# Mixer projections as three fp32r products on split operands, their weights in pairs of ring slots

## The reference

```python
def hybrid_mixer(h, positions, layer, w_in, w_out, ...):
    (q1, q2, k1, k2, va, qb, kb, vb, ob, ib, fb, cq, ckv, kr) = jnp.split(h @ w_in, split_idx, axis=-1)
    out_a = diff_attention_group(q1, q2, k1, k2, va, ...)      # 4 heads, two softmaxes each
    out_b = mlstm_group(qb, kb, vb, ob, ib, fb, ...)           # conv, silu, gates, 6 heads
    out_c = mla_group(cq, ckv, kr, ...)                        # latents, rotary key, 6 heads
    return jnp.concatenate([out_a, out_b, out_c], axis=-1) @ w_out
# layer 0: dense SwiGLU (3584 wide); layer 1: top-2-of-8 expert SwiGLU
```

## Time and profile before

| | us |
|---|---|
| median of 3 runs | 1719.91 (1714.5 to 1721.17) |
| profiled execution | 1717.92 |
| its span in the trace | 1716.1 |
| PE busy | 1512.4 |
| DVE busy | 732.0 |
| ACT busy | 561.5 |
| PEld (weight loads into the array) | 1200.4 |
| POOL busy | 63.2 |

### The profile page before, as it was taken

The page is one execution under the profiler, slowest core; times in us unless marked ns, Lnnn a source line. Parts: engine busy times, 40 slices in busy tenths (PEclk is TensorE's granted clock), DMA queues, the critical chain, the costliest instruction groups (busy, mean ns, idle before and its releaser), DMA issues.

```text
span 1716.1 us, 29819 instructions
## 1 busy us (share of the span) xinstructions
PE 1512.4 (88%) x12054; PEld 1200.4 (70%) x12055; DVE 732.0 (43%) x1058; ACT 561.5 (33%) x777; POOL 63.2 (4%) x66
## 2 busy tenths in 40 slices
PE   5999999999999999856659999989997669999894
PEld 3868878999976776644447875489995458888552
DVE  2263265565534522300018871166772036666212
ACT  2134144444322321100016751056551035554101
POOL 0010000000010001000000000000000000000002
PEclk9999999999999999987879999989999779999997
DMA  9726467545352436699999999997577996555793
GB/s 357 273 95 239 191 245 276 201 176 203 138 192 74 173 147 274 273 424 423 425 425 426 400 378 403 425 369 286 236 279 313 424 424 260 221 221 221 311 426 149
DMA packets 74557, 488.85 MB, mean 285 GB/s; under 512 B 9792, under 2 KB 13920, under 8 KB 16544
## 3 DMA queue, kind: packets, MB, share of 16 engines
q1 hardware_dynamic: 72176, 479.94, 69.7%
q10 hardware_dynamic: 1648, 4.59, 0.8%
q0 software_dynamic: 576, 2.10, 0.4%
HBM read 482.66 MB, written 3.93 MB: 284 GB/s over the span
## 4 chain that ended last, share of the span: by engine, by line
PE 79%; DMA 10%; issue 5%; DVE 3%; ACT 2%; POOL 1%; SPq 1%; ACTq 0%; POOLq 0%; DVEq 0%
PE PG L1370 9%; PE PG L923 6%; PE Y L949 5%; PE PG L1414 5%; PE PG L1480 5%; PE TRB L1414 4%; DMA arena<-in_experts 4%; PE Y L1382 4%; PE Y L1442 4%; DMA ring<-in_experts 4%; PE Y L1211 3%; PE Y L957 3%; PE PG L925 3%; PE TRB L1420 3%; PE PG L1420 3%
## 5 line engine op out<-in xcount | busy, mean ns | idle before, releaser
L1370 PE MATMUL PG<-ring,mixT 128*32 128x128 f32 (+1 forms) x1920 | 116.3, 347 | 61.4 <-issue 56.9
L2381 DVE COPY arena<-TRB 128x64 f32<-128x64 f32 (+1 forms) x70 | 17.6, 251 | 340.3 <-PE TRB L1356 340.3
L1563 ACT ACTIVATE parts<-ring 128x2048 fp32r<-128x2048 f32 x84 | 157.2, 1901 | 4.8 <-PE PG L1480 4.8
L923 PE MATMUL PG<-h_parts,parts 128*128 128x512 f32 x432 | 152.8, 394 | 1.4 <-DVE arena L2260 1.4
L1370 PEld LDWEIGHTS PG<-ring,mixT 128*32 128x32 f32 (+1 forms) x1920 | 89.5, 136 | 91.7 <-issue 77.0
L1563 ACT ACTIVATE rope<-PG 64x128 f32<-64x128 f32 (+2 forms) x84 | 27.2, 324 | 376.5 <-PE PG L1370 352.6
L1370 PE MATMUL PG<-arena,mixT 128*32 128x128 f32 (+1 forms) x1664 | 103.6, 357 | 41.3 <-issue 41.3
L1370 PEld LDWEIGHTS PG<-arena,mixT 128*32 128x32 f32 (+1 forms) x1664 | 79.8, 141 | 69.1 <-issue 55.1
L925 PE MATMUL PG<-h_parts,parts 128*128 128x256 f32 x432 | 121.8, 282 | 0.0
L2245 DVE TENSOR_TENSOR parts<-ring,parts 128x2048 fp32r<-128x2048 f32 x42 | 95.1, 2289 | 32.7 <-ACT parts L1563 32.7
L2365 DVE TENSOR_TENSOR ring_parts<-ring,parts 128x2048 fp32r<-128x2048 f32 x42 | 95.0, 2286 | 22.4 <-PE Y L1433 19.4
(11 more groups left out here) (358 smaller groups left out, 2715.6 us busy)
## 6 DMA issues: line engine op xcount, KB each, us to landing
ring<-in_experts SPq DMA_DIRECT2D x168, 1024.0 KB, 12.2
arena<-in_experts SPq DMA_DIRECT2D x168, 1024.0 KB, 16.3
ring<-in_weights SPq DMA_DIRECT2D x116, 1024.0 KB, 6.3
ring<-in_weights SPq DMA_DIRECT2D x4, 512.0 KB, 4.2
ypairs<-hT ACTq DMA_DIRECT2D x3, 512.0 KB, 5.4
tok<-in_x SPq DMA_DIRECT2D x1, 1024.0 KB, 9.0
result<-scr SPq DMA_DIRECT2D x2, 512.0 KB, 2.6
ring<-in_weights SPq DMA_DIRECT2D x2, 432.0 KB, 6.5
```

Source lines behind the costliest of these rows:

```text
L923: mm(PG[:, m, :].rearrange("p (i t) -> p i t", i=2), w_hi[d % SPLITS][:, c], h_parts[:, :, k, :], start=(k == 0), stop=False, skip_group_c ...
L1370: last = mm(bank[i * n:(i + 1) * n, 0:width], xe[:, k, 0:n], w[k // 4][:, k % 4, i * width:(i + 1) * width], start=(k == 0), stop=(k == KD ...
L1563: return nc.scalar.activation(out_, in_, func, **kw)
```

## The change

h and the mixed rows are kept as hi and lo (h_parts; mix_hi and mix_lo use the same memory later), and the token rows tok become mtok, which uses hT's memory. ACT's shift now writes h_hi, and low_shifted on DVE writes h_lo. Each input and output weight takes two ring slots: SP loads it into the first, part on ACT copies it, rounded to fp32r, into the second ("hi"), and lower on DVE writes weight - hi over the loaded slot. SP skips the "hi" uses; part waits for the landing and for the last reader of the slot that it writes. The latent and the vb weights, which were cut by columns, are cut by rows, so that their products are 364 and 384 columns wide. PE does hi x hi and hi x lo, waits for the low weight, and does lo x hi. Row product D moves from behind the early output products to behind co. part and lower stand at fixed places in ACT's and DVE's programs.

```diff
-        uses.extend(("in", l, key) for key in W_IN_ORDER[a:b])
+        uses.extend((kind, l, key) for key in W_IN_ORDER[a:b] for kind in ("in", "hi"))
...
-        uses.extend(("out", l, c) for c in OUT_ORDER)
+        uses.extend((kind, l, c) for c in OUT_ORDER for kind in ("out", "hi"))
...
-W_IN_ORDER = [(COL_LAT, 256), (COL_LAT + 256, LATW - 256), (COL_Q, 256), (COL_Q + 256, 256), (COL_VA, 256),
+W_IN_ORDER = [(COL_LAT, LATW // 2), (COL_LAT + LATW // 2, LATW // 2), (COL_Q, 256), (COL_Q + 256, 256), (COL_VA, 256),
               (COL_QK, 256), (COL_QK + 256, 256), (COL_QK + 512, 256), (COL_OB, 256), (COL_OB + 256, 128),
-              (COL_VB, 256), (COL_VB + 256, 128)]
+              (COL_VB, BH * BD // 2), (COL_VB + BH * BD // 2, BH * BD // 2)]
+K_HALF = {W_IN_ORDER[0]: (COL_LAT, LATW, 0), W_IN_ORDER[1]: (COL_LAT, LATW, KD // 2),
+          W_IN_ORDER[10]: (COL_VB, BH * BD, 0), W_IN_ORDER[11]: (COL_VB, BH * BD, KD // 2)}
...
-            *[f"pt{u}" for u in range(6)], "rows2", "gt", "mt0", "cols2", "co0", "co1", "mt1", "mt2", "rows3",
+            *[f"pt{u}" for u in range(6)], "rows2", "gt", "mt0", "cols2", "co0", "co1", "rows3", "mt1", "mt2",
...
+        mix_hi, mix_lo = (h_parts[:, i, :, :] for i in range(2))
+        mtok = hT.rearrange("p k t -> p (k t)").rearrange("p (b d) -> p b d", b=TB)
...
-            eng.wait_ge(landed[slot_of[u]], 16 * (u // SLOTS + 1))
+            eng.wait_ge(landed[slot_of[u]], 16 * sum(x[0] != "hi" for x in uses[slot_of[u]:u + 1:SLOTS]))
+
+        def last_reader(kind, a, b):
+
+            if kind == "ada":
+                return tr_full, TR.full(("ada", a, b // 4))
+            if kind == "in" or kind == "hi" and b in IN_ITEM:
+                return pj_full, PJ.full((IN_ITEM[b], a))
+            if kind in ("out", "hi"):
+                return (y_full, 2 + a) if b == OUT_ORDER[-1] else (out_read, (D // SW - 1) * a + OUT_ORDER.index(b) + 1)
+            return split_lo, dense_use(kind, b) + 1
...
+                if kind == "hi":
+                    continue
                 if u >= SLOTS:
...
+                    hi, lo = proj_parts(l, key)
+                    hi_of(key)
                     for i in range(n):
-                        last = fm(bank[:, i * T:(i + 1) * T], s, i * P, P)
+                        for k in range(KD):
+                            for x in (h_hi, h_lo):
+                                mm(bank[:, i * T:(i + 1) * T], hi[:, k, i * P:(i + 1) * P], x[:, k, :],
+                                   start=(i == 0 and k == 0 and x is h_hi), stop=False, skip_group_check=True)
+                    lo_of(key)
+                    for i in range(n):
+                        for k in range(KD):
+                            last = mm(bank[:, i * T:(i + 1) * T], lo[:, k, i * P:(i + 1) * P], h_hi[:, k, :],
+                                      start=False, stop=(k == KD - 1), skip_group_check=True)
                     last.then_inc(pj_full, 1)
...
+                def latents():
+
+                    banks = [take_pj((f"lat{b}", l)) for b in range(TB)]
+                    halves = [proj_parts(l, key) for key in keys[0:2]]
+                    his, los = zip(*halves)
+                    h = KD // 2
+                    for b, bank in enumerate(banks):
+                        for k in range(KD):
+                            if b == 0:
+                                if k % h == 0:
+                                    hi_of(keys[k // h])
+                                pe.wait_ge(h_ready, KD * 2 * l + k + 1)
+                            mm(bank[:, 0:LATW], h_hi[:, k, b * P:(b + 1) * P], his[k // h][:, k % h, :],
+                               start=(k == 0), stop=False, skip_group_check=True)
...
+                    for b, bank in enumerate(banks):
+                        for k in range(KD):
+                            if b == 0:
+                                pe.wait_ge(h_lo_ready, KD * 2 * l + k + 1)
+                            last = mm(bank[:, 0:LATW], h_lo[:, k, b * P:(b + 1) * P], his[k // h][:, k % h, :],
+                                      start=False, stop=(k == KD - 1), skip_group_check=True)
+                        last.then_inc(pj_full, 1)
...
+                for key in keys[10:12]:
+                    hi_of(key)
+                    lo_of(key)
                 for b in range(TB):
                     bank = take_pj((f"vb{b}", l))
-                    tm(bank[:, 0:SW], s0, b, SW)
-                    tm(bank[:, SW:SW + P], s1, b, P).then_inc(pj_full, 1)
+                    tm(bank[:, 0:BH * BD], b, his, los).then_inc(pj_full, 1)
...
+                    hi, lo = proj_parts(l, c)
+                    late = tiles is MIX_LATE
+
+                    def product(w, x, k, j):
+                        return mm(Yk[:, 2 * c + j, :], w[:, k, j * P:(j + 1) * P], x[:, k, :],
+                                  start=(j == 0 and k == 0 and w is hi and x is mix_hi),
+                                  stop=(late and k == MIX_LATE[-1] and x is mix_lo), skip_group_check=True)
+
+                    hi_of(c)
                     for j in range(2):
                         for k in tiles:
-                            last = mm(Yk[:, 2 * c + j, :], ring[:, s, k, j * P:(j + 1) * P], mixT[:, k, :],
-                                      start=(j == 0 and k == 0), stop=(k == MIX_LATE[-1]), skip_group_check=True)
+                            product(hi, mix_hi, k, j)
+                    if not late:
+                        for j in range(2):
+                            for k in tiles:
+                                product(hi, mix_lo, k, j)
+                    lo_of(c)
+                    for j in range(2):
+                        for k in tiles:
+                            last = product(lo, mix_hi, k, j)
+                    if late:
+                        pe.wait_ge(mix_lo_ready, 2 * l + 2)
+                        for j in range(2):
+                            for k in tiles:
+                                last = product(hi, mix_lo, k, j)
                     return last
...
+            def part(l, key):
+                u, n = proj_use(l, key)
+                use_wait(ae, u)
+                if u + 1 >= SLOTS:
+                    ae.wait_ge(*last_reader(*uses[u + 1 - SLOTS]))
+                run(ring_parts[:, slot_of[u + 1], 0:n], ring[:, slot_of[u], :, :].rearrange("p k c -> p (k c)")[:, 0:n],
+                    ACT.Copy).then_inc(proj_hi, 1)
...
+                part(l, W_IN_ORDER[10])
                 at(2)
                 at(3)
+                part(l, W_IN_ORDER[11])
...
-                run(mixT[:, 0:2, :], bank.rearrange("p (a t) -> p a t", a=2), ACT.Copy, scale=gd[:, l:l + 1]).then_inc(free, 1)
+                run(mix_hi[:, 0:2, :], bank.rearrange("p (a t) -> p a t", a=2), ACT.Copy,
+                    scale=gd[:, l:l + 1]).then_inc(mix_hi_ready, 1)
+                part(l, OUT_ORDER[0])
                 ae.wait_ge(*tr_done("gt", l))
...
-            for third in ADA_START:
-                ada_rows(third)
+            ada_rows(ADA_START[0])
+            for key in W_IN_ORDER[0:2]:
+                part(0, key)
+            ada_rows(ADA_START[1])
             shift(0)
...
+            def lower(l, key):
+                u, n = proj_use(l, key)
+                ve.wait_ge(proj_hi, proj_index(l, key) + 1)
+                V.tensor_tensor(ring_parts[:, slot_of[u], 0:n], ring[:, slot_of[u], :, :].rearrange("p k c -> p (k c)")[:, 0:n],
+                                ring_parts[:, slot_of[u + 1], 0:n].bitcast(F32), ALU.subtract).then_inc(proj_lo, 1)
+
+            def low_shifted(n):
+                for k in range(KD):
+                    ve.wait_ge(h_ready, KD * n + k + 1)
+                    V.scalar_tensor_tensor(h_lo[:, k, :], hT[:, k, :], mod[:, n, k:k + 1], h_hi[:, k, :].bitcast(F32),
+                                           ALU.add, ALU.subtract).then_inc(h_lo_ready, 1)
...
+                lower(l, W_IN_ORDER[10])
                 negmaxes("c", 0, 1, 2, 3)
+                lower(l, W_IN_ORDER[11])
...
+                lower(l, OUT_ORDER[1])
+                for name, f, m in (("mt1", slice(5, 7), 2), ("mt2", slice(7, 8), 3)):
+                    bank, free = tr_item(name, l)
+                    n = f.stop - f.start
+                    ve.wait_ge(mix_hi_ready, 5 * l + m)
+                    V.tensor_tensor(mix_lo[:, f, :], bank[:, 0:n * T].rearrange("p (a t) -> p a t", a=n),
+                                    mix_hi[:, f, :].bitcast(F32), ALU.subtract).then_inc(free, 1)
...
+                late = [(name, j, f) for name, f0, n in (("mt3", 2, 2), ("mt4", 4, 1)) for j, f in enumerate(range(f0, f0 + n))]
+                turned = {name: tr_item(name, l)[0] for name in ("mt3", "mt4")}
+                for i, (name, j, f) in enumerate(late):
+                    last = V.scalar_tensor_tensor(mix_hi[:, f, :], turned[name][:, j * T:(j + 1) * T], gml[:, l, i:i + 1],
```

(37 more changed lines are left out.)

144 lines of the change are left out of this document (84 added, 60 removed).

## The result

| | before | after |
|---|---|---|
| median, us | 1719.65 (4 runs, 1714.5 to 1721.17) | 1738.62 (4 runs, 1735.97 to 1740.48) |
| profiled execution, us | 1717.92 | 1735.97 |
| its span | 1716.1 | 1734.2 |

The changed kernel is slower: ratio 1.0111, 95% interval 1.0094 to 1.0128, some 19 us where I had forecast 7 to 8. The time lies in my range, at its upper end.

What follows compares the result with a forecast made beforehand. PE was taken to bound the kernel, busy 88% of the span. Per mixer -16.7 + 4.0 + 2.1 + 8.6 + 2.4 = +0.4, with starts 3.4 and clock 3.6 in all +7.8: 1727 us, range 1706 to 1741.

Steps and rivals of the forecast that it cites:

- Products: PE in each mixer: three fp32r products at 0.119 us replace one fp32 product at 0.432 us, -16.7 us a mixer.
- Rival 4: Split products on PE take 0.144 us and not 0.119, so nothing is saved: 1760 us, chance 4%.
- Copies hidden: Input projections a0 to qk2: weight copies on ACT and subtractions on DVE cost nothing, with 1 to 4 us to spare.
- Rival 3: Copies taken as hidden come late on ACT, PE stops more often and the clock falls again: 1740 us, chance 22%.
- The starts: Mixer starts: latent weights' copy or subtractions delay the chain to hT, +1.4 us in mixer 0, +2.0 in mixer 1.
- Before vb: Ahead of vb products: aT late behind a vb copy, +1.65 us, then low vb weights late, +2.3; 4.0 a mixer.
- Loads behind vb1: Third row product's last weight gets its slot only when vb1 ends: +2.1 us; first output weight lands 16.8 us after vb1.
- ACT behind that load: ACT's copy of the first output weight holds up the gate exponentials: +8.6 us a mixer, the largest term, bounds 0 and 12.
- The end of the mixer: Early and late output products wait for low parts that DVE writes: +2.4 us a mixer.
- The loads for what follows: After the mixer: the dense stage's last ada weight lands at 4.3 us, asked at 4.8, and experts' loads are on time: nothing.
- The sum: Whole kernel: +0.8 us for two mixers, starts 3.4, clock 3.6, together +7.8; 1727 us from the median of 1719.91.
- The clock: One half-clock stretch of about 1.8 us per mixer, behind the 8.6 us stop: +3.6 us in all, bounds 0 and 9.

Runs made afterwards that it cites:

- Experiment 1: Changed kernel with ACT's copy of the first output weight behind the gate exponentials and its DVE subtraction behind the score products: 1717.03 us, ratio 1.0003.
- experiment 10: Changed kernel with seven edits of order, plus products of constants before the last start columns, both mixers' latents and the second pt: 1695.13 us, ratio 0.9864.
- experiment 2: Changed kernel with products of constants where PE waits before vb0, row product C, the third w and the dense stage's first row product: 1732.5 us, ratio 1.0088.
- experiment 6: Changed kernel with ACT's two aT evictions ahead of the first vb copy and low vb weights waited for only where used: 1736.0 us, ratio 1.0100.

## Why the prediction was right or wrong

**Products.** Right: -17.6 and -16.8 us of work for -16.7, at 0.121 us a product. Rival 4 is out.

**Copies hidden.** Right: from a0 to ob1 PE waits nowhere in either profile where it did not before. (Ahead of the prediction I gave the page's busy digits of ACT and DVE in the mixers as 0 to 3; they are 1 to 4 and 2 to 6. The windows of the earlier trace rows, on which the argument rests, are right.) Rival 3, which wanted late copies there, gave nearly the time that came (1740): its late copies did not come, its half clock behind more stops did. That the time lies in my range is luck in this sense: the range was held open by rival 3, not by the forecast's terms.

**The starts.** Mixer 0 +0.7 for +1.4, but +3.5 in the second profile, where the half clock ahead of it is 6.1 us and not 4.1. Mixer 1 +3.4 and, in the second profile, +1.7 for +2.0; 3.1 us of half clock lie in the first one's stretch.

**Before vb.** +1.65 and +2.3 forecast, the idle times are 1.34 and 1.69 us.

**Loads behind vb1.** C waits 5.1 us from vb1's end and not 4.3 (152.0 to 157.13; D's first weight is issued right behind it), +2.9 for +2.1. The output weight lands 18.5 us after vb1's end (170.5 - 152.0) for 16.8.

**ACT behind that load.** From C's end to co +9.4 and +9.3 us with the clock in it, for +8.6 and 1.8. ACT waits 6.12 and 6.56 us for the weight, where I wanted 7 to 9. Experiment 1 takes the stop away alone, and with it 18.6 of the 19 us.

**The end of the mixer.** The stops stand at 1.75 and 2.25 us, in both mixers; co to the end is 1.1 and 2.6 us shorter than before for -2.4.

**The loads for what follows.** Wrong in the first profile: "Nothing", since I took a lone load's 4.3 us. The last ada weight landed 7.6 us after its slot was free, with the transfers still busy (279 GB/s and more in each microsecond from 212 us on), and PE stood 2.81 us. In experiment 1 it came 5.1 us after, with a lull of 115 GB/s ahead of it. But in the second profile of the changed kernel the wait was 1.19 us and this stretch no longer than before, and in experiment 10 the weight came 7.9 us after, also with a lull of 115 GB/s ahead of it. What makes this load late stays open.

**The sum.** 1719.91 + 7.8 is 1727.7 and not 1727. Of the stretches at 528 and 706 us, which I priced at about 1.8, the windows give 1.7 and 1.3 us. Both are small beside the next.

**The clock: the step that failed.** "I count one per mixer, behind the 8.6 us stop: +3.6. Bounds 0 and, if the shorter stops do it too, 9." The first profile has eight stretches in the two mixers where before had one, 13.6 us more, and 4.8 between them; the second 18.8 more in the mixers. Both lie beyond my bound of 9. In the mixers alone the mis-sized term is 10.0 us short, of 10.3 between the forecast's +7.8 and the spans' +18.1; the other terms' errors (work -1.0, stops -2.8, the starts +0.7, the dense row product +2.5, the experts +0.9) nearly cancel, which is in part luck. In the second profile, whose span is 19.1 us above the one before, the term is 15.2 us short, and the others together were forecast 3.9 us too high.

I had looked at single stops and asked which is long enough. What the runs show is that stops of 1.3 to 3 us, each followed by dense work, also bring 0.50, at vb0, at C, at the latents, and not each time. The Trainium skill (TensorE: Matmul & The Clock Gate, "A second HAM failure mode: psum-queue depth-cycling") has a case where short idle times between groups of products, frequent enough, make the clock go down and up; the two traces agree with that rule rather than with the one I had taken, and it should have been the rival.

That the stop is the cause is shown for C and for the latents: there PE fell to 0.50 in all four cases of the changed kernel's two profiles, and stayed at 1.00 in both mixers where fillers stood in the stop (experiments 2 and 10). At vb0 it fell in three of four cases, and two with fillers are few to tell by.

The kernel before could have told me. I passed over a third stretch, in a row product at the start, behind a wait of 2.22 us. It costs 1.7 us and comes in both of its profiles:

```profile
32.17 5.35 PE L866 MATMUL TRB<-ring,ccol 128*32 128x256 f32 x64 [2.22 <-DMA ring<-in_weights]
...
33.00:36.00 3.00, 3.00 (x35) 1.91 (x28) 0.00 (x0) 0.00 (x0) 0.00 (x0) 0.50 1.09 343
```

And the stop before 17.28 us, which I took as a sign against, is there in all 13 profiles of these kernels at 2.75 or 2.76 us: in six of them PE falls to 0.50 within 2 us of it, in seven it does not.

How much of the time the half clock explains is less sure than its place in the account. Fillers took 11.3 us of it away and won 4 to 6 in the median (experiment 2), or 5.9 and won nothing (experiment 10). And experiment 1 brought the kernel back to the time of before with 20.6 us of it left.

What stays open: which of the short stops brings the half clock in a given execution. Two profiles of one program differ in it by up to 5.2 us within a mixer.

## What to carry to other kernels

Where an engine runs in order, a copy that waits for a load belongs behind everything that does not need it: one copy moved was worth 18.6 us, nearly the change's whole loss. Taking work off the engine that bounds gave it more stops here, and of the stops of 1.3 to 3 us many cost granted clock as well as idle time, so count every new stop of a microsecond or more at the clock it may leave behind, not only the longest. And a stop taken away alone may only uncover the next in series, as in experiment 6. Here seven changes of order together made a kernel 1.4% faster than the one before, though not each of them showed a gain by itself.

## What the runs showed of the hardware

- Granted clock: the kernel before gave the same stretches at 0.50 in two profiles, 3.4 us up to the end of mixer 1; the changed one 24.2 and 26.5 us, in part at different places, though most idle times came back within 0.1 us and the longest within 0.6.
- Fillers of constants in a stop kept the clock at 1.00 behind it (C 3.66 for 5.35 us), where they lasted to its end; behind a remainder of 3.4 us without them PE was at 0.50 again (experiment 2, the third w).
- From a slot coming free to the start of the product that its 1 MB load feeds: 5.1 us at C in the changed kernel; for the last ada weight of the dense stage 7.6 and 6.0 us in two profiles of the changed kernel, 5.1 in experiment 1 and 7.9 in experiment 10.
